# A two-layer mixer and transformer block on one core: input and context handed over with features on rows

## The reference, cut to what matters

```python
act_lat = silu(c);  act_ctx = silu(c_ctx)                # vectors of 1024
sh_l, sc_l, gt_l = split(act_lat @ w_ada[0] + b_ada[0], 3)    # w_ada[0] is 1024 x 3072
sh_c, sc_c, _    = split(act_ctx @ w_ada[0] + b_ada[0], 3)
u_lat = rms_norm(x,   norm_g[0]) * (1 + sc_l) + sh_l     # x: 512 x 1024
u_ctx = rms_norm(ctx, norm_g[0]) * (1 + sc_c) + sh_c     # ctx: 256 x 1024
p_lat = u_lat @ mla_w_in                                 # 1024 x 1472
p_ctx = u_ctx @ mla_w_in[:, 256:448]
...                                                      # attention, and all that follows
# rms_norm(v, g) = v * rsqrt(mean(v*v over features) + 1e-6) * g
```

## Time and profile before

| | |
|---|---|
| median of 3 runs | 1284.62 us (1284.25 to 1284.8) |
| the profiled execution, its own time | 1285.15 us |
| its span in the profile | 1283.4 us |
| PE busy | 1271.1 us (99%) |
| PEld / DVE / ACT / POOL busy | 1065.3 / 818.3 / 655.3 / 448.8 us |
| read from and written to device memory | 129.66 MB and 4.72 MB |

### The profile page before, as it was taken

How to read it: one execution, slowest core, us unless ns; L and a number is a source line. 1 busy time by engine, 2 the same in 40 slices (tenths; PEclk the granted TensorE clock), 3 DMA queues, 4 the chain that set the end, 5 groups by cost and what they waited for, 6 DMA issues and landing times.

```text
span 1283.4 us, 17458 instructions
## 1 busy us (share of the span) xinstructions
PE 1271.1 (99%) x6553; PEld 1065.3 (83%) x6553; DVE 818.3 (64%) x1208; ACT 655.3 (51%) x1066; POOL 448.8 (35%) x212
## 2 busy tenths in 40 slices
PE   9999999999999999999999999999999999999998
PEld 4688888889988888888789889888888888888886
DVE  1796788764945457789658335406448678667686
ACT  5543777744523354766655534632355534545341
POOL 0243011137433394522244334344663322333210
PEclk9999999999999999999999999999999999999999
DMA  9972001076332153322223233233354233332301
GB/s 348 322 241 75 11 23 33 18 246 187 97 99 66 34 164 99 99 53 63 65 70 96 83 82 83 78 93 94 96 164 154 84 124 99 107 107 82 115 1 66
DMA packets 181401, 135.43 MB, mean 106 GB/s; under 512 B 10154, under 2 KB 154651, under 8 KB 181324
## 3 DMA queue, kind: packets, MB, share of 16 engines
q1 hardware_dynamic: 181122, 134.34, 34.5%
q10 hardware_dynamic: 202, 0.06, 0.0%
HBM read 129.66 MB, written 4.72 MB: 105 GB/s over the span
## 4 chain that ended last, share of the span: by engine, by line
PE 88%; DVE 4%; ACT 4%; DMA 2%; POOL 1%; issue 1%; ACTq 0%; DVEq 0%; SPq 0%; POOLq 0%
PE psum L2379 27%; PE psum L2381 26%; PE psum L2380 26%; PE psum L2437 2%; PE psum L2593 2%; DMA w_raw<-in_fno_w_in 1%; PE psum L2581 1%; PE psum L2582 1%; POOL w_lo L784 1%; ACT w_hi L903 1%; DVE m_probs L2031 1%; DVE m_turned_lo L2036 0%; PE psum L2530 0%; DMA w_raw<-in_mla_w_out 0%; DMA vec_rows<-in_moba_k_norm_g 0%
## 5 line engine op out<-in xcount | busy, mean ns | idle before, releaser
L784 POOL TENSOR_TENSOR w_lo<-w_raw,w_hi 128x1024 fp32r<-128x1024 f32 x148 | 383.6, 2598 | 641.0 <-ACT w_hi L903 605.7
L2379 PE MATMUL psum<-u_hi,w_hi 128*128 128x512 f32 (+1 forms) x704 | 265.2, 377 | 1.0 <-DVE u_lo L1837 0.6
L2381 PE MATMUL psum<-u_hi,w_lo 128*128 128x512 f32 (+1 forms) x704 | 260.9, 371 | 0.0
L2380 PE MATMUL psum<-u_lo,w_hi 128*128 128x512 f32 (+1 forms) x704 | 260.7, 370 | 0.0
L903 ACT ACTIVATE w_hi<-w_raw 128x1024 fp32r<-128x1024 f32 x148 | 155.0, 1053 | 72.2 <-PE psum L2381 28.1
L2379 PE MATMUL psum<-y_hi,w_hi 128*128 128x512 f32 x416 | 162.2, 390 | 0.0
L2381 PE MATMUL psum<-y_hi,w_lo 128*128 128x512 f32 x416 | 161.9, 389 | 0.0
L2380 PE MATMUL psum<-y_lo,w_hi 128*128 128x512 f32 x416 | 161.9, 389 | 0.0
L2379 PEld LDWEIGHTS psum<-u_hi,w_hi 128*128 128x128 f32 x704 | 132.8, 189 | 23.5 <-POOL w_lo L784 1.2
L2381 PEld LDWEIGHTS psum<-u_hi,w_lo 128*128 128x128 f32 x704 | 132.6, 188 | 23.2
L2380 PEld LDWEIGHTS psum<-u_lo,w_hi 128*128 128x128 f32 x704 | 132.9, 189 | 21.0 <-issue 0.2
(11 more groups left out here) (511 smaller groups left out, 2591.2 us busy)
## 6 DMA issues: line engine op xcount, KB each, us to landing
w_raw<-in_w_in SPq DMA_DIRECT2D x52, 512.0 KB, 3.8
w_raw<-in_w_up SPq DMA_DIRECT2D x32, 512.0 KB, 4.1
down_set<-in_w_down SPq DMA_DIRECT2D x32, 512.0 KB, 4.8
ada_back<-in_w_ada SPq DMA_DIRECT2D x7, 2048.0 KB, 11.2
w_raw<-in_fno_w_in SPq DMA_DIRECT2D x16, 512.0 KB, 3.9
ada_w<-in_w_ada SPq DMA_DIRECT2D x3, 2048.0 KB, 14.3
w_raw<-in_mla_w_in SPq DMA_DIRECT2D x11, 512.0 KB, 5.2
w_raw<-in_mla_w_out SPq DMA_DIRECT2D x8, 512.0 KB, 3.9
```

The costliest lines, as they stand in the source:

```text
L784: pool.tensor_tensor(WL[:, j, :], RAW[:, j % 2, :], f(WH[:, j, :]), ALU.subtract).then_inc(lo_done, 1)
L2379: pe.matmul(out, ah, bh, start=first, stop=False, skip_group_check=more)
L2380: pe.matmul(out, ah, bl, start=False, stop=False, skip_group_check=more)
L2381: return pe.matmul(out, al, bh, start=False, stop=last, skip_group_check=more)
```

## The change

x and ctx are handed over transposed, and all vectors as one 128 x 115 array of columns. So x is loaded straight into `HT` and the context into `CTX`, and no transposes of x, of the vectors or of the context are left. The inverse norms need sums over features, which now lie on partitions: ACT squares the chunks, DVE adds the eight chunks up to one (`XSUM`, `CSUM`), and a matmul with ones sums over the partitions. SP loads the columns and the modulation quarters 0, 2 and 1 ahead of x; quarter 3 comes in two halves behind x. The bias inputs and the identity move to ACT's queue. `ada(3)` is cut into three pieces, with the sum and the spreading of the norms between them. The context's norm is a full 128 x 256 tile (`CRSTD`) made by ACT's square root and DVE's reciprocal. SP issues `gate_load(1)` and all behind it once the context's square sum is made (`in_sum` 2), since the squares lie where that load goes.

```diff
@@ sync
-            sp.dma_start(IDENT[:], d["identity"]).then_inc(s_const, 16)
-            for n in range(2):
-                sp.dma_start(XTOK[:, 2 * n:2 * n + 2, :], ...).then_inc(s_x[n], 16)
-            (AQ[0] in two halves, T5, HOT, mask row, AQ[2], AQ[1], AQ[3])
+            sp.dma_start(COLS[:, 0:NROWS], d["columns"]).then_inc(s_cols, 16)
+            ada_halves(0, s_first)
+            for q in (2, 1):
+                sp.dma_start(AQ[q][:], ada_weights(q)).then_inc(s_adaq[q], 16)
+            for n in range(2):
+                sp.dma_start(HT[:, 4 * n:4 * n + 4, :], d["x"][...]).then_inc(s_x[n], 16)
+            ada_halves(3, s_last)
...
             gate_load(0)
             key_rope_tile()
-            sp.wait_ge(row_ss, TT + 1)
-            sp.wait_ge(x_t, KC)
+            sp.wait_ge(in_sum, 2)
             gate_load(1)
             gate_tile(0)
             gate_tile(1)
@@ scalar
-            (15 DMAs of vectors)
+            (4 DMAs: T5, HOT, mask row, IDENT)
             act.activation(DUMMY[:, 0:1], EPST[:], ACT.Silu)
-            (8 copies of turned x, 4 squares of token rows with sums, square root)
+            act.wait_ge(s_cols, 16)
+            (CACT, CSPLIT as before)
+            act.activation(DUMMY[:, 0:1], EPST[:], ACT.Sqrt)
             ada_row_copy(0, 0, 1)
-            ada_row_copy(1, 2, 2)
             act.wait_ge(s_adaq[1], 16)
-            (4 quarter parts QHI)
+            second_hi(0)
+            second_hi(1)
+            ada_row_copy(1, 2, 2)
+            second_hi(2)
+            second_hi(3)
+            x_squares(0)
+            x_squares(1)
             ada_row_copy(2, 1, 4)
+            x_squares(2)
+            x_squares(3)
+            act.wait_ge(spread_mm, 2)
+            act.activation(RSC[:, 0:TT], bank(0, 2 * TT)..., ACT.Sqrt, ...).then_inc(in_sq, 1)
             split_hi(A0, None, 0)
             (lat_hi 0 to 3, with split_hi(A0, None, 1) after the first)
             ada_row_copy(3, 3, 5)
             act.wait_ge(s_ctx, 16)
-            (2 squares of context rows with sums, square root)
+            act.wait_ge(in_sum, 1)
+            for n in range(2):
+                act.activation(CSQ[:, 4 * n:4 * n + 4, :], CTX[:, 4 * n:4 * n + 4, :], ACT.Square).then_inc(in_sq, 1)
             for c in range(4, KC):
                 lat_hi(c)
             split_hi(A0, None, 2)
-            act.wait_ge(row_ss, 9)
-            (2 scaled context rows)
+            act.wait_ge(spread_mm, 4)
+            act.activation(CRSTD[:], bank(6, TC), ACT.Sqrt, scale=1.0 / D, bias=EPST[:]).then_inc(in_sq, 1)
             act.wait_ge(kv_raw[1], 16)
             split_hi(A0, None, 3)
@@ vector
+            for n in range(2):
+                v.wait_ge(in_sq, 2 * n + 2)
+                a, b = slice(4 * n, 4 * n + 2), slice(4 * n + 2, 4 * n + 4)
+                link(v.tensor_tensor(XSQ[:, a, :], XSQ[:, a, :], XSQ[:, b, :], ALU.add))
+            link(v.tensor_tensor(XSQ[:, 0:2, :], XSQ[:, 0:2, :], XSQ[:, 4:6, :], ALU.add))
+            v.tensor_tensor(XSUM[:], XSQ[:, 0, :], XSQ[:, 1, :], ALU.add).then_inc(in_sum, 1)
+            v.wait_ge(in_sq, 5)
+            (reciprocal, 4 DIAG tiles: before, these stood ahead of QLOW)
...
+            v.wait_ge(in_sq, 7)
+            link(v.tensor_tensor(CSQ[:, 0:4, :], CSQ[:, 0:4, :], CSQ[:, 4:8, :], ALU.add))
+            link(v.tensor_tensor(CSQ[:, 0:2, :], CSQ[:, 0:2, :], CSQ[:, 2:4, :], ALU.add))
+            v.tensor_tensor(CSUM[:], CSQ[:, 0, :], CSQ[:, 1, :], ALU.add).then_inc(in_sum, 1)
...
-                v.tensor_scalar(E[...], turned_ctx(c), MULC[:, c:c + 1], ADAC[:, c:c + 1], ALU.mult, ALU.add)
+                v.scalar_tensor_tensor(E[...], CTX[:, c, :], MULC[:, c:c + 1], CRSTD[:], ALU.mult, ALU.mult)
...
             def ctx_chunks():
+                v.wait_ge(in_sq, 8)
+                link(v.reciprocal(CRSTD[:], CRSTD[:]))
@@ tensor
-            for _ in range(18):
+            for _ in range(12):
                 pe.matmul(bank(6, P), ONES[:], ONES[:], start=True, stop=True)
-            (32 transposes of x, 1 of the vectors)
             ada(0); bias spread; ada(2)
+            turn_row(0, 0); quarter 1 high part with turn_row(1, 2) in its middle; quarter 1 low part
+            ada(3, 0, 4)
+            pe.wait_ge(in_sum, 1)
+            for m in range(TT):
+                mm = pe.matmul(bank(0, 2, 2 * m), XSUM[:, m * P:(m + 1) * P], ONES[:, 0:2], start=True, stop=True)
+            mm.then_inc(spread_mm, 1)
+            ada(3, 4, 6)
+            pe.wait_ge(q_lo1, 4 + TT)
             (4 DIAG matmuls: before, these stood behind ada(2))
+            ada(3, 6, KC)
...
+            for k in range(4):
+                pe.wait_ge(u0_lo, k + 1)
+                lat_step(0, k)
+                if k == 1:
+                    pe.wait_ge(mod_done, 1)
+                    last_columns()
+            pe.wait_ge(lo_done, 2)
+            for k in range(4):
+                lat_step(1, k)
+            (then k = 4 to 7 for both tiles)
             for j in range(2, 4):
                 pe.wait_ge(lo_done, j + 1)
                 for k in range(KC):
                     mm = lat_step(j, k)
-                    if j == 3:
-                        turn_ctx(k)
+                if j == 2:
+                    pe.wait_ge(in_sum, 2)
+                    pe.wait_ge(u0_hi, KC)
+                    pe.matmul(bank(6, TC), ONES[:], CSUM[:], start=True, stop=True).then_inc(spread_mm, 1)
```

More of the change, by code:

```diff
@@ L1575, in _ @@
                 .then_inc(bias_row, 1)
-            v.wait_ge(row_ss, TT + 1)
-            link(v.reciprocal(RSC[:, 0:TT], RSC[:, 0:TT]))
             v.wait_ge(s_const, 16)
-            for m in range(TT):
-                v.tensor_scalar(DIAG[:, m, :], IDENT[:], RSC[:, m:m + 1], None, ALU.mult).then_inc(diag_done, 1)
             link(v.tensor_tensor(SEL4[:], IDENT[0:4, 0:2], IDENT[0:4, 2:4], ALU.add))
@@ L2452, in _ @@
             ada(0)
-            pe.wait_ge(x_copied, KC)
             pe.wait_ge(bias_row, 2)
@@ L2457, in _ @@
             ada(2)
-            pe.wait_ge(diag_done, TT)
+            pe.wait_ge(s_const, 16)
+            turn_row(0, 0)
+            pe.wait_ge(cact_done, 4)
+            for k in range(KC):
+                pe.wait_ge(q_hi1, k // 2 + 1)
+                pe.matmul(ada_row_bank(1)[0:4, :], CSPLIT[:, k, :], QHI[:, k, :], start=k == 0, stop=False)
+                if k == 3:
+                    turn_row(1, 2).then_inc(ada_mm, 1)
+            for k in range(KC):
+                pe.wait_ge(q_lo1, k // 2 + 1)
+                mm = pe.matmul(ada_row_bank(1)[0:2, :], CSPLIT[:, k, 0:2], QLOW[:, k, :], start=False, stop=k == KC - 1)
+            mm.then_inc(ada_mm, 1)
+            ada(3, 0, 4)
+            pe.wait_ge(in_sum, 1)
+            pe.wait_ge(bias_row, 3)
+            for m in range(TT):
+                mm = pe.matmul(bank(0, 2, 2 * m), XSUM[:, m * P:(m + 1) * P], ONES[:, 0:2], start=True, stop=True)
+            mm.then_inc(spread_mm, 1)
+            ada(3, 4, 6)
+            pe.wait_ge(q_lo1, 4 + TT)
             for m in range(TT):
@@ L3155 @@
         if name in vec_of:
-            key = vec_of[name]
-            a = a.reshape(-1, MD if key in ("q_norm", "k_norm") else P)
+            vectors[vec_of[name]] = a.reshape(-1, MD if vec_of[name] in ("q_norm", "k_norm") else P)
+            continue
+        if name in ("x", "ctx"):
+            a = _np.ascontiguousarray(a.reshape(-1, D).T)
         elif a.ndim == 3 and a.shape[0] == 1:
@@ L3161 @@
         d[key] = nc.dram_tensor(f"in_{name}", a.shape, _mybir.dt.from_np(a.dtype), kind="ExternalInput").ap()
+    rows = [_np.tile(vectors[name], (1, 2)) if name in ("q_norm", "k_norm") else vectors[name] for name, _ in VECS]
+    arrays["in_columns"] = _np.ascontiguousarray(_np.concatenate(rows).T)
+    d["columns"] = nc.dram_tensor("in_columns", (P, NROWS), _mybir.dt.float32, kind="ExternalInput").ap()
     for name, a in shape_constants().items():
```

169 lines of the change are left out of this document (48 added, 121 removed).

## The result

The changed kernel takes 1290.31 us in the median of 5 runs (1288.7 to 1291.95), the kernel before 1284.62. The ratio is 1.0045, with a 95% interval of 1.0032 to 1.0059: slower by 0.3 to 0.6%. The profiled execution took 1288.7 us with a span of 1286.9 us, and it is the quickest of the five. Each run's profile gives a mean granted clock: 0.999 in the profiled one, 0.996 and 0.997 in the four others.

What follows compares the result with a forecast made beforehand. PE was taken to bound the kernel; -0.9 (opening) - 1.77 (transposes) + 4.8 (fourth tile) + 0.1 (chunks) = +2.2 us on 1284.62, giving 1287.0 us with rounding up. The 8-in-10 range was 1285.2 to 1289.5 us.

Steps and rivals of the forecast that it cites:

- What bounds the kernel: Whole kernel: PE, busy 99% of the span, sets the end; its shift at the gate tiles' start is the end's shift.
- The fourth tile: Fourth weight tile: PE stands still while root, high part and low part follow the context's sum; +4.8 us.
- The transposes: PE's fourth weight tile: the 16 context transposes go, all gain on PE's path; -1.77 us.
- The opening: Up to the weight tiles: first tile step 1.5 us sooner, less some 0.6 us of new waiting; -0.9 us.
- The context's chunks: Behind the fourth tile: DVE's last context chunk comes slightly after PE needs it; 0 to 0.8 us, taken as 0.1.
- the clock falls in the new gap: Rival, before the fourth tile: PE's idle gap halves the clock, +4.3 us in all, 1288.9 us; chance 0.22.
- the sum without the clock: Opening to gate tiles: all terms with no clock fall give +2.2 us, 1287.0 us forecast.
- SP's queue and late gate tiles: SP's gate loads and bias store issue 7 to 9 us later, cost nothing; rival 2 to 3 us more, chance 0.08.
- The chances: Whole kernel, against a 0.2% threshold: slower 0.49, same 0.44, faster 0.07.

Runs made afterwards that it cites:

- opening_alone: The kernel before with only the change's opening (everything up to u), context part as before: 1284.59 us, ratio 1.0004.
- context_first: Changed kernel with context sum after the third tile's third step, fourth tile split ahead of the root, context chunks before modulation(0): 1286.02 us, ratio 1.0005.
- gap_filled: Changed kernel with 16 matmuls of ones on PE behind the context's sum, the wait itself kept: 1289.15 us, ratio 1.0033.
- before_split_late: The kernel before with one added wait: ACT makes the fourth weight tile's high part only after PE finished the third: 1289.9 us, ratio 1.0043.
- split_ahead: Changed kernel with ACT's high part of the fourth weight tile moved ahead of its wait for the context's sum: 1291.01 us, ratio 1.0050.
- opening_alone_filled: opening_alone with 5, 4 and 8 matmuls of ones on PE in the opening's three waits: 1284.51 us, ratio 0.9998.
- best_with_filler: context_first with modulation quarter 1 loaded and multiplied second, plus 4 matmuls of ones on PE before the first tile step: 1281.9 us, ratio 0.9978.
- all_gaps_filled: gap_filled with 5, 4 and 8 more matmuls of ones on PE in its three opening waits: 1287.26 us, ratio 1.0017.

## Why the prediction was wrong

- **What bounds the kernel**: held. Up to the gate tiles PE is moved by its own waits, its clock and the transposes alone. Behind them the profiles differ by 0.9 us the other way, which isn't shown to be the change's.
- **The fourth tile**: the mechanism was right, the size close. I took 4.8 us; the profile has 4.53, by the four instructions that I named. Its wait alone, put into the kernel before, makes 5.1 us with its clock.
- **The transposes**: I took -1.77 us; at the full clock the tile without them takes 5.62 us against 7.22, so it is -1.6.
- **The opening**: I gave it -0.9 us, and it is 0 (59.79 against 59.78; 1284.59 us alone). The first tile step came at 41.19, not 40.35. It is 0.7 us earlier than before instead of 1.5, and the new waiting ahead of the third tile's end took that back. DVE's additions and ACT's squares ended 0.5 us later than by my sum, PE's eight small passes took 1.05 us where I took 0.8, and DVE began u at 38.32, not 37.5: one of its small modulation instructions took 0.41 us instead of 0.16 and ended as POOL's split of the first weight tile did (35.84 + 2.35 = 38.19). Quarter 3 itself was there 1 us before my estimate, so the landing was not what set it.
- **The context's chunks**: I took 0.1 us; in the changed kernel they cost PE nothing. But they were the next limit, which is why moving the split alone gave nothing: their last low part is done at 71.78 us, as I had worked out (71.3 to 72.1), and without the gap PE wants it near 68. POOL did hold up DVE's additions by the 2 us that I had named (3.34 us against 1.2). I called that hidden, and it is, only as long as PE stands still before the fourth tile.
- **The step that failed** is the clock, which my sum put at nothing: *the clock falls in the new gap* had 0.22, and it is what happens. It fell in the profile of the changed kernel and in that of the kernel before with the late split. Behind the gap it cost 1.6 us where my rival took 2.1. That price came from slow weight loads at the start, and the granted clock reads 1.00 in those stretches (1 to 9 us), so they didn't show what a fall costs. In the median the clock cost 3.1 us. The rest beyond the gap's 1.6 is most likely a low clock in the opening, as the profiles of opening_alone and context_first have it; the four slower executions of the changed kernel have no trace that shows it. The forecast missed by 3.3 us, of which 3.1 are the clock; the rival's 1288.9 missed by 1.4.
- **Luck in the sum without the clock**: 1287.0 was forecast and 1287.26 measured with all gaps filled. But in the profile of gap_filled the context's products start 3.05 us later than before (70.05 against 67.00), where my terms make 2.2: the opening gave 0 instead of 0.9, the transposes 0.17 less, and the gap and the chunks cost 0.4 less than I took. That the end still agrees is in part the spread of executions behind 125 us, where this profile made up 1.4 us against the one of before.
- **SP's queue and late gate tiles**: held at nothing; PE waits for no gate tile.
- **The chances**: slower had 0.49 and came true. The advice of the Trainium skill, TensorE: Matmul & The Clock Gate, the section Why this matters for your kernels, to leave no longer idle gaps between bursts of matmuls, which I had cited with a rival, was the better guide. The trace agrees for the gaps before the fourth tile: 3.94 us in the changed kernel and 3.57 in before_split_late, both with 1.2 GHz behind them. It isn't enough for the opening, where the clock fell behind pieces of 0.48 us and less.

## What to carry to other kernels

When a wait moves into an engine's stream, list what stands behind it there and who waits for that: a root of 0.5 us held a weight split that PE needed, and 1.0 + 2.4 us of other engines' work became PE's. On a PE that is busy 99% of the time, price an idle gap together with the clock behind it, and look at the granted clock of every run, since the median may have a loss that the profiled execution lacks. When removing the first of two waits gives nothing, look for the second one right behind it before dropping the theory: here the split alone gained nothing, the split together with an earlier sum and earlier chunks 4.3 us, and a better order of the loads on top made the kernel faster than before. And look at the trace of a run with filler before you credit the filler: fewer slow runs alone didn't show that it kept the clock.

## What the hardware showed that I had not expected

The clock fell without a long idle piece. In the run split_ahead PE was at 1.2 GHz from 70 to 76 us behind one idle piece of 1.37 us, one of 0.30 and context steps that came every 0.92 us; in context_first from 42 to 50 us behind pieces of 1.3, 1.0 and 2.0 us (ending at 28.9, 33.5 and 41.2 us), between which PE ran mostly modulation matmuls with two output rows. It fell with the waits filled as well: from 45 to 49 us in opening_alone_filled and from 44 to 48 us in best_with_filler, where no idle piece since 17 us was longer than 0.48.

Nor do the idle pieces decide it. The profiles of the changed kernel and of gap_filled have the same three waits as context_first and show 1.00 in the opening; all_gaps_filled has the same filled opening as opening_alone_filled and shows 1.00 throughout. The kernel before, whose PE has idle pieces of at most 1.1 us in the same 50 us, shows 1.00 throughout in its one profile. What makes the clock fall in one execution of the same opening and not in another stays open.
